# A two-block transformer on one core: the heads of three attentions taken in pairs, modulation sums stacked by four

## The reference

```
# first_block, each of 2 layers
z = rms_norm(x, norm_mix[l]) @ w_in[l]       # q 8 heads, k and v 2 heads of 64, hgrn, conv
o_att = block_attention(q_a, k_a, v_a)       # softmax over all 512 keys; 4 query heads share a k/v head
x = x + concatenate([o_att, o_hg, o_cv]) @ w_out[l]
x = x + square(relu(rms_norm(x, norm_mlp[l]) @ w_mlp_in[l])) @ w_mlp_out[l]
# second_block, each of 2 layers
mod = (silu(c) @ w_mod[i] + b_mod[i]).reshape(B, 3, 3, 1024)   # w_mod[i] is 1024 x 9216
x = sandwich(x, ffn, ...); x = sandwich(x, mixer, ...); x = sandwich(x, ffn, ...)
# mixer of layer 0: mla, 16 heads, q and k of 64 + 32, v of 64, causal, blocks of 128 queries
# mixer of layer 1: dilated_attention, for 3 groups (window 128, 512, 2048; dilation 1, 4, 16), 16 heads of 64:
s = einsum('bnqrhe,bnkrhe->bnrhqk', qb, kw) * (E ** -0.5)      # 128 queries, the block and the one before
logits = where(valid, s + bias, -inf);  lse = logsumexp(logits)
o = einsum('bnrhqk,bnkrhe->bnqrhe', exp(logits - lse), vw)
o = sum over groups of softmax(lse over groups) * o_group;  result = o @ w_o
```

## Time and profile before

| | |
|---|---|
| median of 3 runs | 3948.55 us (3941.54 to 3949.09) |
| the profiled execution | 3948.49 us, span 3946.6 us |
| granted TensorE clock, mean | 0.974 of 2.4 GHz |
| TensorE matmuls busy | 3807.9 us (96%), 19232 instructions |
| TensorE weight loads busy | 3088.1 us (78%) |
| VectorE busy | 2311.6 us (59%), 2995 instructions |
| ScalarE busy | 1312.2 us (33%), 1735 instructions |
| GpSimd busy | 814.0 us (21%), 580 instructions |
| DMA | 377.73 MB, mean 96 GB/s |

### The profile page before, as it was taken

One profiled execution on the slowest core, in us unless ns is written; L12 is line 12 of the kernel. 1 busy time (PEld: TensorE's weight loads), 2 busy tenths in 40 slices (PEclk: granted clock), 3 DMA queues, 4 the chain that ended last, 5 costly groups with the idle time before them and its releaser, 6 DMA issues.

```text
span 3946.6 us, 48088 instructions
## 1 busy us (share of the span) xinstructions
PE 3807.9 (96%) x19232; PEld 3088.1 (78%) x19232; DVE 2311.6 (59%) x2995; ACT 1312.2 (33%) x1735; POOL 814.0 (21%) x580
## 2 busy tenths in 40 slices
PE   8998999999899999998899999999999999999999
PEld 6777888767788878886677888788878778777887
DVE  5987555488755555566667545643564554555434
ACT  4454332345432232223553212222233333332222
POOL 2100545311054435552103540000000000000000
PEclk9998999999999999998999999999999999999999
DMA  5112444311154445542214543233312112222331
GB/s 159 59 39 69 146 144 142 93 57 52 53 156 138 140 112 155 144 144 62 63 40 108 155 123 96 72 107 98 98 62 82 61 62 75 67 57 72 107 96 65
DMA packets 557161, 377.73 MB, mean 96 GB/s; under 512 B 30201, under 2 KB 554074, under 8 KB 556938
## 3 DMA queue, kind: packets, MB, share of 16 engines
q1 hardware_dynamic: 556938, 374.65, 32.5%
HBM read 372.44 MB, written 2.17 MB: 95 GB/s over the span
## 4 chain that ended last, share of the span: by engine, by line
PE 83%; DVE 13%; ACT 2%; issue 1%; SPq 0%; DMA 0%; DVEq 0%; ACTq 0%
PE bank L441 62%; PE bank L449 3%; PE bank L484 2%; PE bank L857 2%; PE bank L2242 2%; DVE w_lo L419 2%; PE bank L842 2%; PE bank L2267 1%; PE bank L478 1%; PE bank L479 1%; DVE conv_sum L1193 1%; DVE norm_tmp L1639 1%; PE bank L850 1%; DVE norm_tmp L1633 1%; DVE std L884 1%
## 5 line engine op out<-in xcount | busy, mean ns | idle before, releaser
L441 PE MATMUL bank<-H_hi,w_hi 128*128 128x512 f32 x2384 | 993.9, 417 | 2.9 <-DVE w_lo L419 1.3
L441 PE MATMUL bank<-H_hi,w_lo 128*128 128x512 f32 x2384 | 932.2, 391 | 0.0
L441 PE MATMUL bank<-H_lo,w_hi 128*128 128x512 f32 x2384 | 930.7, 390 | 0.0
L419 DVE TENSOR_TENSOR w_lo<-w_raw,w_hi 128x2048 fp32r<-128x2048 f32 (+3 forms) x285 | 732.3, 2569 | 140.5 <-ACT w_hi L410 124.8
L410 ACT ACTIVATE w_hi<-w_raw 128x2048 fp32r<-128x2048 f32 (+3 forms) x285 | 529.2, 1857 | 305.1 <-DMA w_raw<-in_ffn_w_up 133.6
L441 PE MATMUL bank<-U_hi,w_hi 128*128 128x512 f32 x1376 | 546.8, 397 | 3.4 <-DVE note L916 3.2
L441 PEld LDWEIGHTS bank<-H_hi,w_hi 128*128 128x128 f32 x2384 | 448.0, 188 | 126.0 <-issue 40.6
L441 PE MATMUL bank<-U_hi,w_lo 128*128 128x512 f32 x1376 | 538.6, 391 | 0.0
L441 PE MATMUL bank<-U_lo,w_hi 128*128 128x512 f32 x1376 | 537.9, 391 | 0.0
L441 PEld LDWEIGHTS bank<-H_lo,w_hi 128*128 128x128 f32 x2384 | 448.7, 188 | 100.6 <-issue 20.5
L441 PEld LDWEIGHTS bank<-H_hi,w_lo 128*128 128x128 f32 x2384 | 447.3, 188 | 97.7 <-issue 0.8
(11 more groups left out here) (370 smaller groups left out, 4880.0 us busy)
## 6 DMA issues: line engine op xcount, KB each, us to landing
w_mod_raw<-in_w_mod SPq DMA_DIRECT2D x144, 512.0 KB, 6.4
w_raw<-in_ffn_w_gate SPq DMA_DIRECT2D x88, 512.0 KB, 4.0
w_raw<-in_ffn_w_up SPq DMA_DIRECT2D x88, 512.0 KB, 5.3
w_raw<-in_dil_w_in SPq DMA_DIRECT2D x36, 1024.0 KB, 5.1
w_raw<-in_w_mlp_in SPq DMA_DIRECT2D x32, 1024.0 KB, 5.5
w_raw<-in_w_mlp_out SPq DMA_DIRECT2D x32, 1024.0 KB, 5.3
w_raw<-in_ffn_w_down SPq DMA_DIRECT2D x32, 1024.0 KB, 5.2
w_raw<-in_w_in SPq DMA_DIRECT2D x16, 1024.0 KB, 5.2
```

The lines of the kernel that those rows point to most:

```text
L419: dve.eng.tensor_tensor(WL[u % SLOTS][:, 0:n], RAW[u % SLOTS][:, 0:n], WH[u % SLOTS][:, 0:n].bitcast(F32), ALU.subtract).then_inc(lo_done. ...
L441: mm = pe.eng.matmul(bank[0:m, :], w[:, k, c0:c0 + m], r[:, k, :], start=(k == 0 and i == 0), stop=(k == kt - 1 and i == 2))
```

## The change

- **Heads in pairs.** An item is now a pair of heads (2t, 2t + 1). The scores of both are issued alternately, the first from rows 0 to 63, the second from rows 64 to 127, into two banks (4 and 5; dilated 3 and 4). The padded copies and the clearing of key halves go. MLA's scores keep their 96 rows. The values of both heads are issued alternately as 64-column products into the two halves of bank 3 (dilated: bank 7). The scores of pair j wait for both exponentials of pair j - 1.
- **Turning banks.** Each head of a pair turns in its own bank (6 and 2; dilated 5 and 2), and a turn waits for the copy two before. In the grouped-query layers the last three pairs use bank 6 alone, because the convolution's sums take bank 2. There are four `probs` buffers instead of three.
- **Order.** `pair_steps`: scores of pair j, values of pair j - 2, first turn of pair j - 1, divide of pair j, second turn of pair j - 1. In the dilated attention mix steps stand between them.
- **Divide.** VectorE takes both reciprocals and scales the first head; ScalarE scales the second.
- **Accumulators.** `z`, `mla_q` and `mla_kv` have two banks instead of three, the dilated projections two instead of four. Beside `mla_out` the steps have 12 points instead of 18 and two column tiles instead of three, beside `dil_out` 12 instead of 24 and two instead of four.
- **Modulation.** A tile is now a quarter of the rows (256) of four column tiles, 32 partitions each, brought by four transfers. GpSimd adds the quarter's sum to those before; after four tiles one product with a four-column matrix `FOURS` gives all four columns' sums, so there are 36 products. `c_2` is loaded by four transfers, once beside itself for each 32 partitions.

```diff
-            add_units(("z", l), H, specs, "none", acc=(0, 1, 2))
+            add_units(("z", l), H, specs, "none", acc=(0, 1))
...
-                                  "none" if g or hq else "tiles")
+                                  "none" if g or hq else "tiles", acc=(0, 1) if g or hq else (0, 1, 2, 3))
...
             sp.eng.wait_ge(mod_part.sem, mod_part.next(sp, lag=2))
-            sp.eng.dma_start(MODR[m % 2][:], io["w_mod_2"][l][:, P * t:P * t + P].rearrange("(k p) n -> p k n", p=P)).then_inc(mod_landed[m % 2].sem, mod_landed[m % 2].add(16))
+            for n in range(4):
+                src = io["w_mod_2"][l][256 * part:256 * part + 256, P * (t0 + n):P * (t0 + n) + P].rearrange("(k p) n -> p k n", p=32)
+                sp.eng.dma_start(MODR[m % 2][32 * n:32 * n + 32], src).then_inc(mod_landed[m % 2].sem, mod_landed[m % 2].add(16))
...
+            if part == 0:
+                pool.eng.wait_ge(mod_summed.sem, mod_summed.next(pool, lag=2))
+                pool.eng.tensor_tensor(MODP[:, four % 2], w[:, 0], w[:, 1], ALU.add).then_inc(mod_part.sem, mod_part.add())
+            else:
+                pool.eng.tensor_tensor(w[:, 0], w[:, 0], w[:, 1], ALU.add).then_inc(pool.step.sem, pool.step.add())
+                pool.eng.wait_ge(pool.step.sem, pool.step.made)
+                pool.eng.tensor_tensor(MODP[:, four % 2], MODP[:, four % 2], w[:, 0], ALU.add).then_inc(mod_part.sem, mod_part.add())
...
+            four, part = divmod(m, 4)
+            if part < 3:
+                return
...
-            pe.eng.wait_ge(mod_part.sem, mod_part.next(pe))
-            pe.eng.matmul(banks[7][:, m:m + 1], MODP[:, m % 4], ONES[:, 0:1],
-                                        start=True, stop=True).then_inc(mod_summed.sem, mod_summed.add())
+            pe.eng.wait_ge(mod_part.sem, m + 1)
+            pe.eng.matmul(banks[7][:, 4 * four:4 * four + 4], MODP[:, four % 2], FOURS, start=True, stop=True).then_inc(mod_summed.sem, mod_summed.add())
...
             if kind == "scores":
-                pe.eng.wait_ge(p_ready.sem, p_ready.next(pe, lag=2))
-                b = banks[4 + i % 2]
-                for q, k, c0, add in it["segs"]:
-                    w = k.shape[-1]
-                    mm = pe.eng.matmul(b[:, c0:c0 + w], q, k, start=True, stop=add is None)
-                    if add is not None:
-                        mm = pe.eng.matmul(b[:, c0 + w - P:c0 + w], EYE, add, start=False, stop=True)
-                mm.then_inc(s_ready.sem, s_ready.add())
+                pe.eng.wait_ge(p_ready.sem, p_ready.next(pe, 2, lag=2))
+                both = pairs_[i]["items"]
+                for n in range(len(both[0]["segs"])):
+                    for y in range(2):
+                        q, k, c0, add = both[y]["segs"][n]
+                        b, w = banks[4 + y], k.shape[-1]
+                        mm = pe.eng.matmul(b[:, c0:c0 + w], q, k, start=True, stop=add is None)
+                        if add is not None:
+                            mm = pe.eng.matmul(b[:, c0 + w - P:c0 + w], EYE, add, start=False, stop=True)
+                        if n == len(both[0]["segs"]) - 1:
+                            mm.then_inc(s_ready.sem, s_ready.add())
...
+                normal = pn_act if y else pn_ready
+                pe.eng.wait_ge(normal.sem, normal.next(pe))
+                pe.eng.wait_ge(pt_ready.sem, pt_ready.next(pe, lag=1 if i > 2 * bufs["one"] else 2))
+                for j in range(pairs_[pair]["n"] // P):
...
-                for j, (v, c0, start, stop) in enumerate(it["v"]):
-                    mm = pe.eng.matmul(banks[3][it["rows"], c0:c0 + P], v, bufs["pt"][i % 2 + (2 if i >= bufs["late"] else 0)][:, j * P:(j + 1) * P], start=start, stop=stop)
+                both = pairs_[i]["items"]
+                for j in range(len(both[0]["v"])):
+                    for y in range(2):
+                        v, c0, start, stop = both[y]["v"][j]
+                        mm = pe.eng.matmul(banks[3][HEAD * y:HEAD * y + HEAD, c0:c0 + P], v, turned_probs(bufs, i, y)[:, j * P:(j + 1) * P], start=start, stop=stop)
                 mm.then_inc(pv_ready.sem, pv_ready.add())
...
+            elif kind == "divide":
+                it = pairs_[i]["items"][1]
+                act.eng.wait_ge(inv_ready.sem, inv_ready.next(act))
+                for n, (_, k, c0, _) in enumerate(it["segs"]):
+                    c, part = it["stat"] + n, bufs["pr"][(2 * i + 1) % 4][:, c0:c0 + k.shape[-1]]
+                    signal = pn_act if n == len(it["segs"]) - 1 else act.step
+                    act.eng.activation(part, part, ACT.Identity, scale=RS[:, c:c + 1]).then_inc(signal.sem, signal.add())
                     act.eng.wait_ge(signal.sem, signal.made)
...
+                first, second = pairs_[i]["items"]
+                dve.eng.wait_ge(p_ready.sem, p_ready.next(dve, 2))
+                for it, signal in ((second, inv_ready), (first, dve.step)):
+                    c, n = it["stat"], len(it["segs"])
+                    dve.eng.reciprocal(RS[:, c:c + n], RS[:, c:c + n]).then_inc(signal.sem, signal.add())
+                    dve.eng.wait_ge(signal.sem, signal.made)
+                for n, (_, k, c0, _) in enumerate(first["segs"]):
+                    c, part = first["stat"] + n, bufs["pr"][2 * i % 4][:, c0:c0 + k.shape[-1]]
+                    signal = pn_ready if n == len(first["segs"]) - 1 else dve.step
+                    dve.eng.tensor_scalar(part, part, RS[:, c:c + 1], None, ALU.mult).then_inc(signal.sem, signal.add())
...
+        def pair_steps(n, j):
+
+            turns = [("turn", 2 * j - 2), ("turn", 2 * j - 1)] if 1 <= j < n + 1 else []
+            return [("scores", j)] * (j < n) + [("values", j - 2)] * (j >= 2) + turns[0:1] + [("divide", j)] * (j < n) + turns[1:2]
+
+        def turn_bank(bufs, pair, y):
+
+            return banks[2 if y and pair < bufs["one"] else 6]
...
+                        rows = slice(HEAD * y, HEAD * y + HEAD)
+                        keys = Z[rows, ZK, :] if y == kv else KSW[rows, :]
+                        items.append({"segs": [(Z[rows, t, b * P:(b + 1) * P], keys, 0, None)], "stat": (2 * t + y) * NB + b,
+                                      "v": [(Z[:, ZV, kb * P + kv * HEAD:kb * P + kv * HEAD + HEAD], b * P, kb == 0, kb == NB - 1) for kb in range(NB)]})
...
-            n = 4 if g else 8
+            n = 2 if g else 4
             mixes = [("mix", k) for k in range(6)]
             steps_ = [("bias", half) for half in range(1 if g else 2)] + [("keys", j) for j in range(0 if g else 2)]
-            for s in range(n + 2):
-                steps_ += [("scores", s)] * (s < n) + [("turn", s - 1)] * (1 <= s < n + 1) + [("values", s - 2)] * (s >= 2)
-                if g == 0 and hq and s < 5:
-                    steps_ += mixes[s:s + 1] if s < 4 else mixes[4:]
+            for j in range(n + 2):
+                mixing = mixes[2 * j:2 * j + 2] if g == 0 and hq else []
+                steps_ += [("scores", j)] * (j < n) + mixing[0:1] + [("values", j - 2)] * (j >= 2)
+                steps_ += ([("turn", 2 * j - 2)] + mixing[1:2] + [("turn", 2 * j - 1)]) if 1 <= j < n + 1 else mixing[1:2]
             if g == 2:
...
+                pe.eng.wait_ge(dil_s_used.sem, dil_s_used.next(pe, 2, lag=2))
+                h4, blocks = dil_blocks(c, 2 * s)
+                t = h4 // 2
                 for b, c0, w in blocks:
                     k1 = (b + 1) * P
-                    mm = te.matmul(banks[4][:, c0:c0 + w], DQ[two][r:r + HEAD, t, b * P:(b + 1) * P], DK[two][r:r + HEAD, t, k1 - w:k1],
-                                   start=True, stop=True)
-                mm.then_inc(dil_s.sem, dil_s.add())
+                    for y in range(2):
+                        r = HEAD * y
+                        mm = te.matmul(banks[3 + y][:, c0:c0 + w], DQ[two][r:r + HEAD, t, b * P:(b + 1) * P], DK[two][r:r + HEAD, t, k1 - w:k1],
+                                       start=True, stop=True)
+                        if b == blocks[-1][0]:
+                            mm.then_inc(dil_s.sem, dil_s.add())
...
                 for b, c0, w in blocks:
                     for x in range(w // P):
                         kb = b + 1 - w // P + x
-                        mm = te.matmul(banks[7][r:P, b * P:(b + 1) * P], DV[two][:, kb, h4 * HEAD:(h4 // 2 + 1) * P],
-                                       DT_[i % 2][:, c0 + x * P:c0 + (x + 1) * P], start=(x == 0), stop=(x == w // P - 1))
+                        for y in range(2):
+                            mm = te.matmul(banks[7][HEAD * y:HEAD * y + HEAD, b * P:(b + 1) * P], DV[two][:, kb, (h4 + y) * HEAD:(h4 + y + 1) * HEAD],
+                                           DT_[y][:, c0 + x * P:c0 + (x + 1) * P], start=(x == 0), stop=(x == w // P - 1))
                 mm.then_inc(dil_v.sem, dil_v.add())
...
-                    pe_pair(pe, first, weave)
+                    pe_pair(pe, first, weave, 2)
...
```

(7 more changed lines are left out.)

324 lines of the change are left out of this document (145 added, 179 removed).

## The result

| | before | after |
|---|---|---|
| median | 3948.06 us (4 runs) | 3894.53 us (4 runs, 3891.53 to 3896.38) |
| ratio | | 0.9866, 95% interval 0.9853 to 0.9879 |
| profiled span | 3946.6 us | 3889.7 us |
| TensorE busy | 3807.9 us | 3678.6 us |
| VectorE busy | 2311.6 us | 2135.0 us |

The change makes the kernel 53.5 us faster. The forecast was 112 faster, 3836, with a range of 3798 to 3885: half of it came, and the time lies above the range. The busy time of TensorE fell by 129 us (151 were forecast), but the time in which it is not busy grew from 138.7 to 211.1 us.

What follows compares the result with a forecast made beforehand. TensorE's instruction stream, 83% of the chain, was taken to bound the kernel. Grouped-query -24, latent -15, dilated -53, modulation -21 and prologue +1 sum to -112: from 3948.5 to 3836 us, range 3798 to 3885.

Steps and rivals of the forecast that it cites:

- The latent attention: Latent attention: 18.0 us of products go and the turning bank's wait shrinks; 15 us saved, between 3 and 29.
- Modulation: Modulation products: 144 one-column products become 36, 23.8 us of TensorE's stream, of which 21 reach the end.
- the tail: Last dilated chunk's steps, woven into the output projection beside fewer column tiles: a cost of 10 us (0 to 20).
- a stage where only TensorE counts: Dilated attention: TensorE's stream alone sets the time, so 65.8 us less 10 and 2.5 gives 53 saved.
- It never was over 86% here; at 86% the stage takes 139: Grouped-query layers: VectorE's busy share caps the gain at 11 us; 12 taken per layer, 24 in all.
- covered: Modulation: GpSimd's extra sum on 108 tiles hides in its 118 us of waiting; without that cover 54 us.
- B: Whole kernel: the gain sticks in the other engines because a pair arrives in a lump; 3880 us, chance 0.20.
- D: Attention stages: a pair's scores wait for both exponentials of the pair before, making it slower; 3968 at 1.5 us, chance 0.03.
- C: Whole kernel: the whole stream gain of 151.1 us arrives, less tail 10 and prologue 1; 3808 us, chance 0.15.
- E: Grouped-query scores: row halves don't overlap at 512 columns, 0.40 us lost per pair; 3850 us, chance 0.07.
- the 150 us window: Grouped-query attention of layer 0, 98 to 248 us: to shrink to about 138 with VectorE near 87%.
- A: Whole kernel: the forecast's own sum, 3836 us, own range 3815 to 3860, chance 0.55.

Runs made afterwards that it cites:

- both reliefs: The changed kernel with 28 of 62 convolution taps and GpSimd's work for 16 modulation tiles left out in the grouped-query stages: 3859.19 us, ratio 0.9786.

## Why the prediction was wrong

**Step by step.** The prices of the single steps on TensorE were right, and so was the prologue (+1 forecast, 1.5 in the trace). The latent attention's 17.3 are soft. Against the other two executions of the code before they are 10 to 12, for the forecast 15, inside its bounds. Modulation was forecast at 21 and measured alone at 11: outside the grouped-query stages it gave what its products cost (6.1, 12.3, 2.7 and 2.1 in the table), inside them it lost. Two terms failed, the dilated and the grouped-query one, and the loss by the modulation belongs to the second.

**Dilated: 53 forecast, 29.1 in the stage less 6.5 in the tail, 23 found.** The step that failed is "a stage where only TensorE counts". VectorE is at half on average, but a first-group pair gives it two heads' logits at once (4.6 us in the rows above; the expectations say 5.5), with a weight split of 2.3 behind, and the mix's product of 0.69 stood behind both. Average load says nothing on a lump. With the second head taken later the stage gives 58.1, less 5.7 in the tail: 52. That this meets the forecast's 53 is partly luck, since the stage alone was to give 63 and the tail to cost 10: both were 4 to 5 too large, and the two errors cancel. The accumulator banks' 2.5 were 1.9 by the waits.

**Grouped-query: 24 forecast, 4 lost, which is nothing within the scatter.** The step was "It never was over 86% here; at 86% the stage takes 139". VectorE's share was no constant: the window's 150 us hold 123.6 busy us, 82%, in a stage that has not become shorter. Its list got later, and its lateness counted for more. GpSimd's sums, which I called covered since GpSimd itself waits 118 us in the earlier trace rows, block VectorE while they run: the cover was looked for on the wrong engine. That costs 20 us in the changed kernel and 9 in the one before; the modulation alone loses 13 in these stages, by one execution of each. And a delay of VectorE that half reached the end before reaches it whole now. My reading of this is that the pairs leave no item of slack (both score banks, ScalarE's divide, copies and values hang on one another); it is argued, not shown. With both reliefs the stages are 19.2 and 15.3 shorter. What share each of the couplings (score banks, divide, bank 2) has stays open: the orders tried moved the waits and hardly the stages.

**What no step had: the clock.** No term said that a TensorE that stands still runs slower afterwards. 22 of the 151 us of stream that should have gone did not show as less busy time, 19 of them in the dilated attention, where the granted clock fell from 1.00 to 0.97 and some 12 of the 19 are the clock. Filling three waits there gave 11 us. The rows read before the forecast had it: the mix in the earlier trace rows takes 1.98 after a wait of 2.91 where the same step takes 1.09 in the earlier trace rows. I read the wait and not the duration. The granted clock there was 0.50:

```profile
3508.40:3510.40 2.00, 2.00 (x17) 1.67 (x17) 0.00 (x0) 1.32 (x2) 0.00 (x0) 0.50 0.00 0
```

**The rivals.** B named the lump of two maxima and two exponentials, and its total was near (3880 for 3894), but it had only 0.20, and the nearness is luck: it gave the dilated attention 40 and the latent attention nothing, where 23 and 10 to 17 came, and the grouped-query layers 8, where nothing came. D's wait exists (17.2 us when the exponential is put later) but is 3.4 us in the changed kernel. C and E are out. The signs by which I meant to recognise the case told it: the 150 us window at 82% instead of 87, the dilated window at 548 instead of 520, and a wait of 3.1 us on a pair's scores where A had none above 1.

## What to carry to other kernels

When one engine's stream gets shorter, look for the others' lumps, not their shares: list what each engine does between two steps that TensorE needs, in order, and price the longest such stretch. A saving that stacks two heads' work into one step of the list should split that step again on the engines that don't profit, unless the bank between them is needed at once. Count a GpSimd operation as work of VectorE wherever VectorE is on the path. A wait of TensorE can cost more than its length: the 3.6 us here cost an estimated 6.5.

## What the runs showed of the hardware

Row halves of TensorE run together at 512 columns in fp32, started 0.01 us apart. After 4.04 us in which no product started TensorE ran at 0.50 of its clock for about 5.8 us; with 24 transposes in the gap it ran at 1.00. A VectorE operation of 0.69 us took 2.17 beside GpSimd, one of 0.55 took 1.38, and GpSimd's sum of some 0.5 took 2.38 beside VectorE's weight split. GpSimd's sums in the two grouped-query stages made VectorE's same operations there 16 us longer in one kernel and 18 in the other.
